# A gated recurrence by decay levels: levels of one and two tokens and the diagonal merged into one level over blocks of four

## What is computed

```python
q = jax.nn.silu(q_in.astype(jnp.float32))
log_f = jnp.logaddexp(jnp.log(lb), jnp.log1p(-lb) + jax.nn.log_sigmoid(f_in.astype(jnp.float32)))
k = -jnp.expm1(log_f)
v = i_in.astype(jnp.float32)
def step(state, xs):
    qc, lfc, kc, vc = xs
    a = jnp.cumsum(lfc, axis=2)
    rel = a[:, :, :, None, :] - a[:, :, None, :, :]
    decay = jnp.exp(jnp.where(causal, rel, -jnp.inf))
    scores = jnp.einsum('bhtd,bhtsd,bhsd->bhts', qc, decay, kc)
    o = jnp.einsum('bhts,bhsv->bhtv', scores, vc) + jnp.einsum('bhtd,bhdv->bhtv', qc * jnp.exp(a), state)
    ...
o = rmsnorm(o, norm_gain)
gate = jax.nn.silu(g_in.astype(jnp.float32)).reshape(b, s, HGRN_HEADS, HGRN_DV)
return (o * gate).reshape(b, s, HGRN_HEADS * HGRN_DV).astype(q_in.dtype)
```

## Time and profile before

| what | us |
|---|---|
| median of 3 runs (lowest to highest) | 2850.87 (2850.46 to 2851.14) |
| the profiled execution: time | 2851.14 |
| the profiled execution: span | 2849.6 |
| PE, DVE, ACT busy | 2745.1, 1445.1, 1168.2 |

### The profile page before, as it was taken

The page is one execution under the profiler, slowest core; times in us unless marked ns, Lnnn a source line. Parts: engine busy times, 40 slices in busy tenths (PEclk is TensorE's granted clock), DMA queues, the critical chain, the costliest instruction groups (busy, mean ns, idle before and its releaser), DMA issues.

```text
span 2849.6 us, 33259 instructions
## 1 busy us (share of the span) xinstructions
PE 2745.1 (96%) x12786; PEld 2081.6 (73%) x12786; DVE 1445.1 (51%) x1658; ACT 1168.2 (41%) x1520; POOL 12.9 (0%) x20
## 2 busy tenths in 40 slices
PE   8999899999999999999999999999999998999896
PEld 6888677778888888888888888787888784434342
DVE  4444355656655555555556644677654563312122
ACT  4444355653444444444444644545444341000001
POOL 0000000000000000000000000000000000000000
PEclk9999999999999999999999999999999999999999
DMA  8765844556556555555555575545465449999997
GB/s 286 291 217 198 307 145 167 185 207 236 207 186 227 185 190 191 191 189 183 189 190 177 191 266 201 201 161 191 171 204 185 148 163 365 427 427 426 427 427 318
DMA packets 115647, 672.70 MB, mean 236 GB/s; under 512 B 12061, under 2 KB 17613, under 8 KB 40656
## 3 DMA queue, kind: packets, MB, share of 16 engines
q1 hardware_dynamic: 85984, 612.52, 58.8%
q10 hardware_dynamic: 27264, 46.58, 4.6%
q0 software_dynamic: 2288, 12.08, 1.2%
HBM read 647.51 MB, written 28.35 MB: 237 GB/s over the span
## 4 chain that ended last, share of the span: by engine, by line
PE 85%; DMA 6%; DVE 4%; ACT 3%; issue 1%; DVEq 1%; ACTq 0%; SPq 0%; PEldq 0%; PEld 0%
PE PS L315 23%; PE PS L317 23%; PE PS L316 22%; PE PS L1988 8%; DMA WIDE<-in_w_up 3%; DMA WIDE<-in_w_gate 2%; DMA WIDE<-in_w_down 2%; DVE LO L273 1%; PE PS L339 1%; PE PS L1926 1%; ACT HI L271 1%; PE PS L1443 1%; PE PS L2085 1%; PE PS L925 0%; PE PS L1597 0%
## 5 line engine op out<-in xcount | busy, mean ns | idle before, releaser
L273 DVE TENSOR_TENSOR LO<-RAW,HI 128x1024 fp32r<-128x1024 f32 x760 | 921.8, 1223 | 844.3 <-ACT HI L271 840.3
L315 PE MATMUL PS<-HI,XH 128*128 128x512 f32 x3040 | 1208.5, 398 | 23.1 <-DVE LO L273 15.0
L317 PE MATMUL PS<-HI,XL 128*128 128x512 f32 x3040 | 1187.3, 391 | 0.0
L316 PE MATMUL PS<-LO,XH 128*128 128x512 f32 x3040 | 1186.2, 390 | 0.0
L271 ACT ACTIVATE HI<-RAW 128x1024 fp32r<-128x1024 f32 x760 | 794.5, 1057 | 788.0 <-PE PS L317 691.7
L315 PEld LDWEIGHTS PS<-HI,XH 128*128 128x128 f32 x3040 | 572.7, 188 | 147.8 <-DVE LO L273 19.4
L317 PEld LDWEIGHTS PS<-HI,XL 128*128 128x128 f32 x3040 | 572.2, 188 | 121.1
L316 PEld LDWEIGHTS PS<-LO,XH 128*128 128x128 f32 x3040 | 573.2, 189 | 118.1 <-issue 2.9
L1988 PE MATMUL PS<-WIDE,XS 128*64 128x512 f32 x1024 | 229.0, 596 | 21.6 <-DMA WIDE<-in_w_up 13.5
L1988 PEld LDWEIGHTS PS<-WIDE,XS 128*64 128x64 f32 x1024 | 75.0, 137 | 159.9 <-issue 159.4
L1988 PE MATMUL PS<-WIDE,Y 128*64 128x512 f32 x512 | 116.5, 597 | 8.8 <-ACT Y L2042 4.8
(11 more groups left out here) (351 smaller groups left out, 1361.9 us busy)
## 6 DMA issues: line engine op xcount, KB each, us to landing
RAW<-in_w_in SPq DMA_DIRECT2D x132, 1024.0 KB, 4.9
RAW<-in_w_mlp_in SPq DMA_DIRECT2D x64, 1024.0 KB, 4.8
RAW<-in_w_mlp_out SPq DMA_DIRECT2D x64, 1024.0 KB, 4.8
WIDE<-in_w_gate SPq DMA_DIRECT2D x64, 1024.0 KB, 22.8
WIDE<-in_w_up SPq DMA_DIRECT2D x64, 1024.0 KB, 18.5
WIDE<-in_w_down SPq DMA_DIRECT2D x64, 1024.0 KB, 20.9
RAW<-in_w_out SPq DMA_DIRECT2D x32, 1024.0 KB, 4.8
RAW<-in_xattn_wkv SPq DMA_DIRECT2D x32, 1024.0 KB, 4.8
```

The lines of the kernel that those rows point to most:

```text
L273: dve.tensor_tensor(r["lo"][:, hl, :], r["raw"](k), r["hi"][:, hl, :].bitcast(F32), ALU.subtract).then_inc(lo_done, 1)
L315: pe.matmul(o, xh, wh, start=kt == 0, stop=False)
L316: pe.matmul(o, xh, wl, start=False, stop=False)
L317: mm = pe.matmul(o, xl, wh, start=False, stop=kt == kn - 1)
```

## The change

The levels of 2 and 1 and the diagonal go. A new level 0 serves all pairs within blocks of four tokens, diagonal included. Its reference is the mean of the second and third token's sums (`MID` holds their sum). Since within a block any pair may occur, queries and keys need full factors of their own: `EQ`, of 1024 elements, for the queries, in the memory that `QF` also uses, and `EE[0]` for the keys. `exponents_of_four` has one addition of 256 and one fused operation of 1024 (SCALAR_TENSOR_TENSOR) on VectorE and two exponentials of 1024 on ScalarE; `factors` has two products of 1024. The load of `QF` can't stand in step 2 any more; `gate_load` in step 24 issues it once the products of level 0 have been made and, in pass 0, all stores issued so far have landed. The steps of seven levels are written out: 7, 9, 11, 13, 16, 19 and 22, each with its products a step later; the end of a pass starts a step earlier.

```diff
-        MASK = work("mask", 6656, 1024, 8)
+        MASK = work("mask", 6656, 768, 6)
...
+        MID = work("mid", 7424, 256).rearrange("p (b n) -> p b n", n=1)
+        EQ = Y[:, 0:1024]
...
-        levels = [32, 16, 8, 4, 2, 1, 0, 64, 128]
+        levels = [32, 16, 8, 4, 0, 64, 128]
...
             def log_sum():
...
-                if g == 0:
-                    all_stored()
-                ld[2].inc(act.dma_start(QF, cols_of(PROJ2, g * 512 + 4096)), 16)
...
+            def gate_load():
+
+                act.wait_ge(s_pe.h, exp_done[levels.index(0), "p"])
+                if g == 0:
+                    all_stored()
+                ld[2].inc(act.dma_start(QF, cols_of(PROJ2, g * 512 + 4096)), 16)
+
+            def exponents_of_four(n):
+
+                e = EE[n % 2]
+                av, ev_ = (x.rearrange("p (b n) -> p b n", n=4) for x in (AA, e))
+                dve.tensor_tensor(MID, av[:, :, 1:2], av[:, :, 2:3], ALU.add)
+                dve.drain()
+                dve.wait_ge(s_pe.h, exp_done[n - 2, "p"])
+                act.wait_ge(s_dve.h, V(dve.scalar_tensor_tensor(out=ev_, in0=MID.to_broadcast([P, 256, 4]), scalar=0.5, in1=av,
+                                                                op0=ALU.mult, op1=ALU.subtract)))
+                act.activation(EQ, e, ACT.Exp, scale=-1.0)
+                act.drain()
+                A(act.activation(e, e, ACT.Exp))
...
             def factors(n):
                 H = levels[n]
+                dve.wait_ge(s_act.h, exp_done[n])
                 if not H:
+                    dve.tensor_tensor(EQ, EQ, QQ, ALU.mult)
+                    exp_done[n, "f"] = V(dve.tensor_tensor(EE[n % 2], EE[n % 2], KK, ALU.mult))
                     return
...
             def products(n):
                 H = levels[n]
-                lft, rgt = (EE[n % 2], EE[n % 2]) if H else (KK, QQ)
-                if H:
-                    pe.wait_ge(s_dve.h, exp_done[n, "f"])
+                lft, rgt = EE[n % 2], EE[n % 2] if H else EQ
+                pe.wait_ge(s_dve.h, exp_done[n, "f"])
...
-            for n in range(len(levels)):
-                k = 7 + 2 * n
+            at_block = [7, 9, 11, 13, 16, 19, 22]
+            for n, k in enumerate(at_block):
                 steps[k] = [lambda n=n: masked(n - 1)] if n else []
                 if n + 1 < len(levels):
                     steps[k].append(lambda n=n: exps_of(n + 1))
                 steps[k].append(lambda n=n: factors(n))
                 steps[k + 1] = [lambda n=n: products(n)]
-            last = 8 + 2 * len(levels)
-            steps[last - 1] = [lambda: masked(len(levels) - 1)]
-            steps[last] = [out_products]
-            steps[last + 1] = [out_squares]
-            steps[last + 2] = [out_norm]
-            steps[last + 3] = [out_gate]
-            steps[last + 5] = [out_T]
+            steps[24] = [lambda: masked(len(levels) - 1), gate_load]
+            steps[25] = [out_products]
+            steps[26] = [out_squares]
+            steps[27] = [out_norm]
+            steps[28] = [out_gate]
+            steps[30] = [out_T]
```

More of the change, by code:

```diff
@@ L1401, in exponents @@
                 if not H:
+                    exponents_of_four(n)
                     return
@@ L1419, in factors @@
                 H = levels[n]
+                dve.wait_ge(s_act.h, exp_done[n])
                 if not H:
+                    dve.tensor_tensor(EQ, EQ, QQ, ALU.mult)
+                    exp_done[n, "f"] = V(dve.tensor_tensor(EE[n % 2], EE[n % 2], KK, ALU.mult))
                     return
                 ev_, qv, kv = blocks_of(H, EE[n % 2], QQ, KK)
-                dve.wait_ge(s_act.h, exp_done[n])
                 dve.tensor_tensor(ev_[:, :, H:2 * H], ev_[:, :, H:2 * H], qv[:, :, H:2 * H], ALU.mult)
@@ L1453, in masked @@
                     return
-                mk = MASK[:, {64: 0, 32: 1, 16: 2, 8: 3, 4: 4, 2: 5, 1: 6, 0: 7}[H], :].bitcast(U32).unsqueeze(1).to_broadcast([P, 4, P])
+                mk = MASK[:, {64: 0, 32: 1, 16: 2, 8: 3, 4: 4, 0: 5}[H], :].bitcast(U32).unsqueeze(1).to_broadcast([P, 4, P])
                 dve.memset(SMALL[:, 500:501], 0.0)
@@ L2268, in constants @@
     q, k = np.arange(P)[None, :], np.arange(P)[:, None]
-    levels = [(q // (2 * h) == k // (2 * h)) & (k % (2 * h) < h) & (q % (2 * h) >= h) for h in (64, 32, 16, 8, 4, 2, 1)]
-    levels = np.stack(levels + [q == k]).astype(np.float32)
+    levels = [(q // (2 * h) == k // (2 * h)) & (k % (2 * h) < h) & (q % (2 * h) >= h) for h in (64, 32, 16, 8, 4)]
+    levels = np.stack(levels + [(q // 4 == k // 4) & (k <= q)]).astype(np.float32)
     return {"ident": np.eye(P, dtype=np.float32), "onehot": onehot, "maskrows": maskrows, "band": band,
```

## The result

| kernel | median of runs (lowest to highest), us | profiled span | pass 0, pass 1 |
|---|---|---|---|
| before | 2851.06 (2850.46 to 2852.46, 7 runs) | 2849.6 | 113.98, 114.09 |
| changed | 2859.52 (2858.76 to 2861.56, 7 runs) | 2858.0 | 117.81, 118.45 |

The ratio is 1.003, with a 95% interval of 1.0021 to 1.004: slower, and clear of noise. A pass is measured as in the earlier trace rows, from the transposes behind its first block to the same place one pass on; pass 1 ends where the second block of the next stage starts. The passes lost 3.8 and 4.4 us, 8.2 together, nearly the whole of it.

A forecast was written before the change was run, and what follows sets the result against it. TensorE was taken to bound the passes, VectorE nearly as tight. Waits less saved products (+4.5 us) and low clock (+3.0) gave +7.5 on 2850.87: 2858.4 us, eight in ten from 2854.0 to 2862.0.

The forecast's parts named there:

- What leaves TensorE: Two levels of products leave each pass: 1.8 us per level, 3.6 per pass, 7.2 in all.
- Up to step 12: Early steps of each pass: nothing moves, so the waits at steps 8 and 10 stay.
- Step 13: VectorE's addition (0.4 us) and fused operation (1.14) replace two subtractions; 0.35 more, inside 0.9 of slack: no wait.
- Step 16: Level 0's factors late: products start 9.80 us after block 16's start (S), and TensorE idles 4.4 us.
- step 20: Products of the 128 level, whose factors are in step 19: TensorE idles 1.6 us before them.
- step 23: Products of the last level, factors in step 22: no wait, slack 0.3 us.
- Idle time together: Each pass, added waits against saved products: loses 2.2 us; both passes +4.5 us.
- The clock: Clock falls to 0.50 behind the 4.4 us wait in each pass: 1.5 us each (0 to 1.7), +3.0 in all.
- The gate load: Moved from step 2 to 24: hidden by 0.2 us or more; 5 us in pass 0 if it takes twice as long.
- The row of 2.33 us: Earlier profile: first matmul behind 2.33 us of idle took 0.50 us, as at full clock; cited for the clock holding.
- That the clock holds: Rival: in the passes the clock holds, or falls where TensorE is idle anyway; 2855.4 us, chance 0.20.
- That VectorE keeps up: Rival: factors are ready when TensorE is, four products of 1.8 us are gained; 2843.5 us, chance 0.08.

The follow-up runs named there:

- the last two runs: e9_split_step (2844.11 us) and e10_late_transposes (2842.57 us), both reorderings built on the changed kernel.
- the spare products: Changed kernel with 16 spare 128x128 products in TensorE's queue ahead of the wait for level 0's factors; 2855.42 us.
- e9_split_step: Changed kernel with level 0's factors first in step 15, level 64's exponents in step 16, last levels at 18 (factors first) and 21; 2844.11 us.
- e8_before_factors_first: Kernel before, nine levels, each step reordered to factors, copies, next level's exponents (level of one token keeps its order); 2863.12 us.
- e2_factors_first_16: Changed kernel with step 16 in the order copies, factors of level 0, exponents of level 64; 2854.17 us.
- e6_every_two: Changed kernel with its seven levels one in every two blocks (steps 7 to 19), end of pass three blocks sooner; 2855.71 us.
- e10_late_transposes: e9_split_step with the transposes of the result in step 30 in place of 29; 2842.57 us.

## Why the prediction was right, point by point

The forecast was 2858.4 us, and 2859.5 was measured; +7.5 against +8.5. The mechanism stood as it was put, and of three terms one was too small. The two passes account for 8.2 of the 8.5 us.

**What leaves TensorE.** Right: products at 1862.75 and the next block at 1864.45, 1.70 us apart; six full levels and a short one. That the algebra saves this time where it is not given back is shown by the last two runs.

**Up to step 12.** The waits at steps 8 and 10 stayed at 1.62 and 1.13 us in pass 0. **Step 13.** No wait, as said, but with less room than I had. The addition of 256 elements took 0.68 from start to start, not 0.4; the fused operation 1.15, as taken. The factors ended at 1861.83 + 0.68 = 1862.51, 0.24 us ahead of the products. VectorE's rows, copies to factors:

```profile
1859.40 0.60 DVE L1408 TENSOR_TENSOR WORK<-Y 128x256 f32<-128x256 f32 x1
1860.08 1.22 DVE L1411 SCALAR_TENSOR_TENSOR Y<-WORK,Y 128x1024 f32<-128x1024 f32 x1
1861.23 0.68 DVE L1446 TENSOR_TENSOR Y<-Y,WORK 128x512 f32<-128x512 f32 x1
1861.83 0.68 DVE L1447 TENSOR_TENSOR Y<-Y,WORK 128x512 f32<-128x512 f32 x1
```

**Step 16.** S + 9.80 was expected; block 16 started at about 1864.45 + 2.83 = 1867.28 and the products at 1877.14, S + 9.86. The last product ahead of them started at 1872.51 and would have been followed 0.23 later, so 4.40 us were lost, against 4.4 expected; the profile's 4.24 counts from that product's modelled end. The rows to lay beside the earlier trace rows: eviction, the late LO piece, the second wide product and the products.

```profile
1867.50 1.27 ACT L493 ACTIVATE WORK<-PS,SMALL 128x512 f32<-128x512 f32 x2 [2.07 <-PE PS L317]
...
1870.37 1.22 DVE L273 TENSOR_TENSOR LO<-RAW,HI 128x1024 fp32r<-128x1024 f32 x1 [3.50 <-ACT HI L271]
...
1875.87 1.22 DVE L1443 TENSOR_TENSOR Y<-Y,WORK 128x1024 f32<-128x1024 f32 x1
...
1877.14 3.47 PE L1464 MATMUL PS<-Y 128*128 128x128 f32 x16 [4.24 <-DVE Y L1443]
1880.37 0.47 PE L315 MATMUL PS<-HI,XH 128*128 128x512 f32 x1
...
1890.27 2.05 PE L1464 MATMUL PS<-Y 128*128 128x128 f32 x16 [1.46 <-DVE Y L1447]
```

VectorE is idle for 3.50 us ahead of the LO piece and TensorE for 4.24 behind it: two engines wait in turn on an order, while neither is short of time. The wait at step 20 is 1.46, from 1.6; none at step 23.

**Idle time together.** +4.5 was expected. Pass 0 is 3.83 us longer, of which the low clock is 1.42 (products take 3.23 us to the next block, not 1.81); 2.4 are left, against 2.2. Pass 1 gives 4.36 less 2.3, 2.1. Right.

**The clock.** +3.0 was expected, 1.5 per pass and 1.7 at most. Pass 0: 1.4. Pass 1: 4.67 us of work at 0.50, 2.3 us lost, over my upper end. This is the term that was mis-sized. I took the length of the low stretches (3.2 and 3.4 us) from two waits of 2.1 and 2.6 us (the stretch behind the 2.1 is 3.4 us long too, all of it work, and cost 1.7 and not 1.5); in pass 1 the clock fell 2.1 us into the wait (1990.71 to 1992.8), while the wait had 2.1 more to go, and stayed low for 6.8. That a stretch can be as long as that stood in the trace of the kernel before, at 359.2 to 366.1, and the rows that I used did not show it. The clock thus cost 1.4 + 2.3 = 3.7 us in the two passes, against 3.0, and the spare products brought back 4.1 us of time; with 4.5 of idle time it makes the 8.2 that the passes lost.

The row of 2.33 us was read rightly: the clock stayed at 1.00 for the 12 us behind it. As evidence it was weak. The same wait, 2.3 us in every run, has a low stretch behind it in four of the other eleven profiles.

**The gate load.** Hidden, as said. ScalarE waited 1.77 us for the store and the load was issued at 1904.63 (about 1904.2 expected, 4.7 ahead of 1908.9); the sigmoid started at 1911.99 straight behind its table load. The wait at the transposes is 1.18 in pass 0 and 1.10 in pass 1, so at most 0.1 us comes from it.

```profile
1904.63 0.42 ACTq L1402 DMA_DIRECT2D Y<-proj  x1
1905.15 1.06 ACT L271 ACTIVATE HI<-RAW 128x1024 fp32r<-128x1024 f32 x1 [1.77 <-DMA xkv<-WORK]
```

**The rivals.** That the clock holds did not happen in either pass; its price was right, 2855.4, which is what the spare products gave (2855.42). That VectorE keeps up did not either; the condition that I gave for it, that the LO piece must come sooner than the eviction allows, is met in e9_split_step by another road: there the wide factors stand ahead of the eviction and ahead of the next exponents, and the gain is real. The range, 2854 to 2862, held the time.

## What to carry to other kernels

A queue that is half idle can still be the one everything waits for. Before a step is moved in a stream that splits its own operands, write down for each engine what stands ahead of it that itself hangs on the last block: here a free block between two levels bought nothing, since the LO piece in front of the step waited for that block. Put into each step first what the next engine needs, but see whether a longer loop over two engines closes through what comes last (8.07 us for 7.24 in e8_before_factors_first). And keep waits of a dense TensorE stream short: one of over 2 us may be paid a second time at half clock, and spare products in the wait are cheaper than the low clock behind it.

## What the runs showed of the clock

Of the waits inside the passes, none of the ones up to 1.7 us was followed by a granted clock of 0.50. Of those between 2.2 and 2.9 us some were and some not: 2.27 held and 2.25 fell in the two passes of one run (e2_factors_first_16), 2.25 fell and 2.59 held in another (e6_every_two), and in that one the two waits of 2.87 differ too. All from 3.1 us up were, or the clock fell within the wait. So which of the middle ones fall is not settled by their length.

Three waits ahead of the passes, where the edits don't reach, say the same. One of 2.3 us at about 43 had a fall behind it in 4 of the 12 profiles, one of 2.1 at about 1603 in 7, and one of 2.6 at about 295 in all twelve. The last shows that the first product behind a wait does not tell: it took 0.79 us in the kernel before and 0.50 in e10_late_transposes, and yet the clock fell there as well, 1.1 us later. That product and the stretch behind it:

```profile
296.03 0.50 PE L315 MATMUL PS<-HI,XH 128*128 128x512 f32 x1 [2.60 <-DVE LO L273]
...
297.40:300.40 3.00, 3.00 (x8) 2.31 (x7) 0.00 (x0) 0.00 (x0) 0.00 (x0) 0.50 1.06 425
```

Nor does a fall need a wait. At about 360 the clock fell in all twelve profiles during 3.6 to 4.0 us of small products (128x15) or within 1 us behind them, with no idle time that the timeline shows; in the kernel before it stayed down for 6.8 us, with TensorE busy throughout:

```profile
359.40:366.00 6.60, 6.60 (x19) 5.33 (x20) 4.31 (x12) 2.44 (x4) 0.00 (x0) 0.50 0.50 156
```

Up to the end of pass 1 the twelve profiles hold fifty low stretches. 48 last 3.4 us and two 6.8, this one and the one in pass 1 of the changed kernel. A fall is thus paid by how much of its stretch is work: 1.4 us in pass 0 of the changed kernel, where part of it lay in the wait, and 2.3 in pass 1.

They also tell why runs of one kernel differ. The twelve profiles enter pass 0 between 1811.03 and 1813.62, though what comes before is the same in all but the size of one load. The five with 6.8 us of low clock up to there enter at 1811.03 to 1811.86, the two with 10.2 at 1811.93 and 1812.17, and the five with 13.7 at 1812.58 to 1813.62: the order is that of the low time, without an exception. That this is the whole of the spread was not tried apart.

The Trainium skill, on the page "TensorE: Matmul & The Clock Gate", section "HAM oscillation — how this bites in real kernels", describes a kernel whose idle gaps throttle it again and again. The two falls in the changed kernel agree with it, and the run with the spare products is this case's measure of what they cost, 1.4 and 2.1 us of pass.
